# A state space layer with its chunk matrices read from a table of lags, turned states copied by ScalarE, and its output kept with channels on partitions

## What is computed

```python
def s5_bidirectional(u, a_re, a_im, log_dt, b_re, b_im, c_re, c_im, d_skip):
    # u: (B, S, 512) in 32 groups of 16 channels, 64 complex states per group, two directions
    y = ut * d_skip
    for d in range(N_DIRS):
        a_bar = exp(lam * dt); b_bar = B * (a_bar - 1.0) / lam
        bu = einsum('sbgc,gpc->sbgp', ut, b_bar)                       # complex
        _, xs = lax.associative_scan(_scan_op, (a_el, bu), reverse=(d == 1), axis=0)
        y = y + einsum('sbgp,gcp->sbgc', real(xs), c_re[d]) - einsum('sbgp,gcp->sbgc', imag(xs), c_im[d])
    return y
...
        y = jax.nn.gelu(y)
        y = y * jax.nn.sigmoid(jnp.einsum('bsc,ce->bse', y, w_glu[l]) + b_glu[l])
        ssm = y * jax.nn.silu(z_ssm)
        merged = jax.nn.sigmoid(g_attn) * jnp.einsum('bsc,cd->bsd', attn, w_branch_attn[l]) \
               + jax.nn.sigmoid(g_ssm) * jnp.einsum('bsc,cd->bsd', ssm, w_branch_ssm[l])
```

## Time and profile before

| | us |
|---|---|
| median of three runs | 4124.12 (4119.46 to 4124.37) |
| profiled execution | 4137.53 |
| its span | 4135.7 |
| TensorE busy in the span | 3700.5 |
| loop over groups (`te_s5`) | 420.9 to 1111.6 |
| transposes and gate (`te_glu`) | 1111.6 to 1176.5 |
| branch products (`te_br`) | 1554.9 to 1777.0 |

### The profile page before, as it was taken

One profiled execution on the slowest core, in us unless ns is written; L12 is line 12 of the kernel. 1 busy time (PEld: TensorE's weight loads), 2 busy tenths in 40 slices (PEclk: granted clock), 3 DMA queues, 4 the chain that ended last, 5 costly groups with the idle time before them and its releaser, 6 DMA issues. The chain is left out here.

```text
span 4135.7 us, 35726 instructions
## 1 busy us (share of the span) xinstructions
PE 3700.5 (89%) x12787; PEld 2003.3 (48%) x12787; DVE 1692.5 (41%) x4152; ACT 1021.0 (25%) x2529; POOL 1003.2 (24%) x1396
## 2 busy tenths in 40 slices
PE   4999999999999889989999967888879973899997
PEld 3744666666545544444444444445545541444443
DVE  4766232233354572336655555333333341112211
ACT  3211111111210450012344444333212210222221
POOL 0377774000000680000000024544420003111111
PEclk8999999999999999999999988999989986999999
DMA  3234423222154003222310000001002213999997
GB/s 140 74 132 150 140 102 115 91 74 74 63 191 138 31 11 127 76 92 72 113 34 23 11 6 1 1 0 62 1 33 92 82 62 120 313 314 327 330 316 232
DMA packets 116436, 450.87 MB, mean 109 GB/s; under 512 B 25587, under 2 KB 40435, under 8 KB 104732
## 3 DMA queue, kind: packets, MB, share of 16 engines
q1 hardware_dynamic: 91324, 360.91, 24.4%
q0 software_dynamic: 19456, 67.15, 5.8%
q10 hardware_dynamic: 5472, 20.45, 1.4%
HBM read 335.10 MB, written 113.36 MB: 108 GB/s over the span
## 5 line engine op out<-in xcount | busy, mean ns | idle before, releaser
L140 PE MATMUL pst<-arena 128*128 128x512 f32 (+3 forms) x6618 | 2710.3, 567 | 97.4 <-DVE arena L156 35.4
L140 PEld LDWEIGHTS pst<-arena 128*128 128x128 f32 x6618 | 1248.7, 200 | 1430.1 <-issue 1270.4
L145 PE MATMUL pst<-arena 128*128 128x128 f32 x2211 | 336.3, 292 | 203.5 <-DVE arena L244 52.5
L162 POOL TENSOR_TENSOR arena<-arena 128x128 f32<-128x128 f32 (+7 forms) x880 | 429.5, 488 | 70.1
L162 DVE TENSOR_TENSOR arena<-arena 128x1 f32<-128x1 f32 (+8 forms) x1185 | 402.2, 339 | 83.3 <-ACT arena L2175 22.6
L145 PEld LDWEIGHTS pst<-arena 128*128 128x128 f32 x2211 | 271.2, 149 | 335.4 <-issue 117.0
L1228 POOL TENSOR_SCALAR arena<-arena 128x384 f32<-128x384 f32 (+1 forms) x128 | 151.8, 1205 | 703.3 <-DVE arena L1220 703.0
L151 ACT ACTIVATE arena<-pst,arena 128x128 f32<-128x128 f32 (+1 forms) x630 | 246.5, 486 | 157.8 <-PE pst L145 155.1
L2122 POOL TENSOR_SCALAR arena<-arena 128x512 f32<-128x512 f32 (+3 forms) x160 | 216.5, 1374 | 281.0 <-DVE arena L162 252.3
L2229 PE MATMUL pst<-arena 128*128 128x256 f32 (+1 forms) x576 | 155.0, 393 | 83.1 <-ACT arena L150 42.5
L165 DVE TENSOR_SCALAR arena<-arena 128x1 f32<-128x1 f32 (+10 forms) x569 | 141.7, 249 | 186.0 <-DMA arena<-in_bc 71.6
(11 more groups left out here) (197 smaller groups left out, 2403.9 us busy)
## 6 DMA issues: line engine op xcount, KB each, us to landing
arena<-in_w_exp SPq DMA_DIRECT2D x48, 3072.0 KB, 12.3
arena<-in_w_ada SPq DMA_DIRECT2D x48, 512.0 KB, 4.9
rotd<-arena POOLq DMA_DIRECT2D x32, 512.0 KB, 4.0
arena<-rotd SPq DMA_DIRECT2D x32, 512.0 KB, 4.5
arena<-sgd SPq DMA_DIRECT2D x16, 1024.0 KB, 8.3
arena<-pwd SPq DMA_DIRECT2D x32, 432.0 KB, 3.5
pwd<-arena SPq DMA_DIRECT2D x16, 576.0 KB, 5.0
h2d<-arena SPq DMA_DIRECT2D x17, 512.0 KB, 2.9
```

Source lines behind the costliest of these rows:

```text
L140: x = t.do.matmul(o, l, r, start=(i == 0), stop=(i == len(pairs) - 1))
L145: x = t.do.transpose(o, i, ident[0:i.shape[0], 0:i.shape[0]])
L162: own(v, s).tensor_tensor(o, a, b, op).then_inc(*inc(s, *event))
```

## The change

Five things.

1. **M from a table of lags.** M depends on the distance of two tokens only. For each four groups `te_lag` makes the 16x16 blocks of all distances with eight matmuls (128 moving columns, output 16 x 128), ScalarE and VectorE copy and add them (`ac_lag`, `ve_lag`), SP stores 16 x 240 values per group in `hkd`, and eight loads with overlapping rows read M back (`sp_s5_blocks`). The first seven calls stand among the first 32 projection tiles, after the tiles in `LAG_AT`; the eighth opens `te_s5`. The 16 small matmuls of each group, the padded B with its store and loads, and Ms are gone.
2. **Turned states by ScalarE.** `te_s5_states` makes two products of 256 columns; ScalarE copies the bank with its halves exchanged (`ac_s5_turned`, two copies of 64 partitions x 512).
3. **Output with channels on partitions.** `te_s5_out` has M, CA and QA as the stationary operand and 256 chunks as columns: five matmuls. Gelu runs on each group's 128 x 256 (`ac_s5_out`), SP stores it in `ytd` and loads it back so that a partition holds a channel, with its tokens ordered (t, n): 8 tokens of a chunk outermost, 256 chunks innermost. The 64 transposes and 16 strided copies of the gate are gone.
4. **Reading that layout.** The gate and the branch product take their 512 moving columns as `by_token`: 64 chunks x 8 tokens, the tokens innermost, 256 elements (1024 bytes) apart. VectorE's last pass of the gate reads yT and writes ssmT in the same pattern.
5. **Order.** The group loop is shifted so that the states of g + 1 are made before the output of g. Three table buffers instead of two. The gate goes by token range first (`u, m = n // 4, n % 4`), and its last pass waits for the four gate tiles of its range, since ssmT lies over yT.

```diff
+LAG_AT = [0, 2, 6, 12, 17, 22, 27]
...
+        def te_lag(t, q4):
+            CAs, b1 = CA2[q4 % 2], b1s[q4 % 2]
+            t.wait_ge(*at("mat_ve", "QA", q4))
+            t.wait_ge(*(at("lag_ac", "H", q4 - 1) if q4 else at("u_ac", "Ug", 30)))
+            t.wait_ge(*at("lag_ve", "H", q4 - 1))
+            for g in range(4):
+                for d in range(2):
+                    x = t.do.matmul(bank(d)[0:16, g * 128:(g + 1) * 128], b1[:, 2 * g + d, :],
+                                    CAs[:, g, 160 * d:160 * d + 128], start=True, stop=True)
+            x.then_inc(*inc("lag_pe", "H", q4))
...
-                b1, b2, x2 = Bb[:, 0, :, :], Bb[:, 1, :, :], Bb[:, 2, :, :]
+                CAs, b1, b2, x2 = CA2[q4 % 2], b1s[q4 % 2], Bb[:, 0, :, :], Bb[:, 1, :, :]
+                v.wait_ge(*at("lag_pe", "H", q4 - 2))
+                if q4 == 1:
+                    v.wait_ge(*at("u_pe", "Ug", 30))
...
+            for k in range(8):
+                src = bass.AP(tensor=hkd.tensor, offset=4 * q4 * 3840 + 112 - 16 * k, ap=[[240, 16], [3840, 4], [1, 128]])
+                s.do.dma_start(Mq[q4 % 2][16 * k:16 * k + 16], src).then_inc(*dma(f"ld_m{q4 % 2}", "M", q4))
...
-            for s in range(8):
-                t.do.matmul(bank(0)[:, 16 * s:128], Bpad[i][:, 0, 112 - 16 * s:240 - 16 * s],
-                            CA[:, 0, 0:128 - 16 * s], start=(s == 0), stop=False)
-            for s in range(8):
-                x = t.do.matmul(bank(0)[:, 0:16 * (s + 1)], Bpad[i][:, 1, 112 - 16 * s:240 - 16 * s],
-                                CA[:, 1, 128 - 16 * s:144], start=False, stop=(s == 7))
...
-                t.do.matmul(bank(2 + d)[:, 0:256], BPT[i][:, d, 0:128], u_, start=True, stop=True)
-                t.do.matmul(bank(2 + d)[:, 256:512], BPT[i][:, d, 128:256], u_, start=True, stop=True
-                            ).then_inc(*inc("s5_pe", "v", g, d))
+                x = t.do.matmul(bank(2 + g % 2)[:, 256 * d:256 * d + 256], BPT[g % 2][:, d, :], u_, start=True, stop=True)
...
+            mm(t, y_bank(g), [(Mq[g // 4 % 2][:, g % 4, :], Ug[:, g, :])] +
+               [(A_[:, d, lo:lo + 128], Gs[:, r, d, d:d + 256])
+                for d, lo in ((0, 16), (1, 0)) for r, A_ in enumerate((CA, QA))]).then_inc(*inc("s5_pe", "y", g))
...
+        def sp_s5_channels(s, g):
...
+            s.do.dma_start(yT[m][p:p + 16], ytd[g].rearrange("(t c) n -> c t n", t=8)).then_inc(*dma("ld_yT", "yT", g))
...
+        def by_token(x, u):
+
+            return x[:, :, 64 * u:64 * u + 64].rearrange("p t n -> p n t")
...
-                mm(t, bank(4 + u), [(w3[:, k, m * 128:(m + 1) * 128], yT[:, k, u * 512:(u + 1) * 512])
-                                    for k in range(4)]).then_inc(*inc("glu_pe", "glu", n))
+                mm(t, in_chunks(bank(4 + m)), [(w3[:, k, m * 128:(m + 1) * 128], by_token(yT[k], u)) for k in range(4)]
+                   ).then_inc(*inc("glu_pe", "glu", n))
...
-                tt(v, "glu_ve", o, o, yT[:, m, us], MUL)
                 v.wait_ge(*at(f"ld_z{n % 2}", "zs", n))
-                tt(v, "glu_ve", o, o, stg[n % 2], MUL, "ssm", n)
+                tt(v, q, o, o, stg[n % 2], MUL)
+                v.wait_ge(*at("ld_yT", "yT", G - 1))
+                v.wait_ge(*at("glu_pe", "glu", 4 * u + 3))
+                tt(v, q, by_token(ssmT[m], u), in_chunks(o), by_token(yT[m], u), MUL, "ssm", n)
...
-                    mm(t, bank(2 * u + 1), [(BW[d % 2][:, 4 + k, :], ssmT[:, k, us]) for k in range(4)]
+                    mm(t, in_chunks(bank(2 * u + 1)), [(BW[d % 2][:, 4 + k, :], by_token(ssmT[k], u)) for k in range(4)]
```

More of the change, by code:

```diff
@@ L581, in pw_stored @@
         def pw_stored(e, q4):
-            for k in range(4):
+            for k in range(3):
                 e.wait_ge(*at(f"st_pw{k}", "pw", q4))
@@ new lines, in ac_lag, with ve_lag @@
+        def ac_lag(a, q4):
+            o = Hs[q4 % 2]
+            two = [bank(d)[0:16, :].rearrange("p (g n) -> p g n", g=4) for d in range(2)]
+            a.wait_ge(*at("lag_pe", "H", q4))
+            a.wait_ge(*at("u_pe", "Ug", 30))
+            a.wait_ge(*at("st_hk", "H", q4 - 2))
+            a.do.activation(o[:, :, 112:240], two[0], ACT.Copy).then_inc(*inc("lag_ac"))
+            a.do.activation(o[:, :, 0:112], two[1][:, :, 0:112], ACT.Copy).then_inc(*inc("lag_ac", "H", q4))
+        def ve_lag(v, q4):
+            q, o = "lag_ve", Hs[q4 % 2][:, :, 112:128]
+            v.wait_ge(*at("ld_sgn", "dcol"))
+            tt(v, q, dd, bc(ident[0:16, 0:16], 1, [16, 4, 16]), bc(dcol[0:16, 4 * q4:4 * q4 + 4], 2, [16, 4, 16]), MUL)
+            v.wait_ge(*at("lag_ac", "H", q4))
+            tt(v, q, o, o, bank(1)[0:16, :].rearrange("p (g n) -> p g n", g=4)[:, :, 112:128], ADD)
+            tt(v, q, o, o, dd, ADD, "H", q4)
@@ L655, in ve_mat @@
                     tt(v, q, o, o, x_, SUB, *(["QA", q4] if d == 1 else []))
+                if q4:
+                    ve_lag(v, q4 - 1)
         def po_rot(p):
@@ L789, in te_s5_out @@
         def te_s5_out(t, g):
-            i = g % 2
             _, CA, QA = pw_views(g)
-            t.wait_ge(*at("s5_ve", "M", g))
+            t.wait_ge(*at(f"ld_m{g // 4 % 2}", "M", g // 4))
             t.wait_ge(*at("s5_ve", "G", g))
-            t.wait_ge(*(at("s5_ac", "Y", g - 1) if g else at("u_ac", "Ust", 12)))
-            for h in range(2):
-                o = bank(4)[:, h * 128:(h + 1) * 128]
-                t.do.matmul(o, Ug[:, g, h * 128:(h + 1) * 128], Ms[i], start=True, stop=False)
-                for d, lo in ((0, 16), (1, 0)):
-                    for r, A_ in enumerate((CA, QA)):
-                        x = t.do.matmul(o, Gs[:, r, d, h * 128 + d:h * 128 + d + 128], A_[:, d, lo:lo + 128],
-                                        start=False, stop=(d == 1 and r == 1))
@@ L832, in te_s5 @@
         def te_s5(t):
+            te_lag(t, 7)
             te_s5_first(t, 0)
@@ L877, in sp_s5 @@
         def sp_s5(s):
-            sp_s5_load(s, 0)
-            sp_s5_load(s, 1)
+            for g in range(3):
+                sp_s5_pw(s, g)
+                if g < 2:
+                    sp_s5_rot(s, g)
+            sp_lag(s, 7)
+            sp_s5_blocks(s, 0)
             for n in LATE[0]:
@@ L2765, in tensor @@
                 te_proj(t, n)
+                if n in LAG_AT:
+                    te_lag(t, LAG_AT.index(n))
             te_s5(t)
```

289 lines of the change are left out of this document (145 added, 144 removed).

## The result

| | before | after |
|---|---|---|
| median | 4124.12 (4119.46 to 4124.37) | 4183.16 (4175.88 to 4197.16) |
| profiled execution | 4137.53 | 4179.35 |
| its span | 4135.7 | 4177.6 |

The changed kernel is slower: the ratio is 1.015, with a 95% interval of 1.0121 to 1.0179. The median of after is of four executions.

The account below looks back on a forecast made before the run. TensorE's own stream was taken to bound the kernel; loop -144, table of lags +20, strided reads +64 and +128, gate ends +3 and +8 gave +79 on 4124, so 4203 us, range 4075 to 4235.

Parts of the forecast that it names:

- The strided reads: Gate and branch matmuls reading 1024 bytes apart: 1.0 us more each, +64 us for the gate and +128 for the branch.
- the sum: Whole kernel: all terms added, -144 + 20 + 64 + 128 + 3 + 8 = +79 us.
- The moving stream that keeps its pace: Rival, gate and branch: strided reads cost nothing extra, the 192 us fall away, total 4011; chance 0.16.
- reads half as slow: Rival, gate and branch: part of the read delay overlaps the array's work, total 4107; chance 0.14.
- lines far apart cost more: Rival, gate and branch: 1024-byte steps cost more than 32-byte ones, total 4395; chance 0.03.
- The late tables: Rival, before the loop: VectorE's table steps grow and TensorE waits, 5 to 10 us on top; no separate chance.
- The loop: Group loop: fewer TensorE matmuls save 4.50 us a group, -144 us for 32, new period 17.0 us.
- The table of lags: First tiles to loop: 64 added matmuls, waits for VectorE's tables and the handover, +20 us (14 to 30).
- The ends of the gate: Before and behind the gate: TensorE waits for weights, +3 us at the head and +8 at the other end.
- The head: Before the gate: TensorE idles for its weights and comes back at the lower clock, +3 us.

Follow-up runs that it names:

- step1: Kernel after with gate, its last VectorE pass and branch product reading 512 tokens contiguously, in wrong order; 0.433 us a record, total not comparable.
- step8: Kernel after with gate and branch moving operands read 8 elements (32 bytes) apart, last VectorE pass contiguous, wrong token order; 0.927 us a record, total not comparable.
- keep: Kernel after with only the table of lags and turned states kept; output, transposes, gate and branch as before; 4011.9 us, ratio to before 0.9718.
- keep_tab: As keep, but VectorE's wait for the end of te_u stands before the first write of CA, not the whole step; 4000.78 us, ratio to before 0.9688.

## Why the prediction was right, and where its numbers were off

**The strided reads** decided, as the sum had it, and `step1` shows that the reads are what costs. Their size was off: the term is "500 ns a record, two records a matmul, 1.0 us on top of 0.86". Measured are 0.88 (1.74 to 1.745 against 0.86), +56 and +112 instead of +64 and +128. The row it came from, the weight load of 315 ns in the earlier trace rows, has a step of 32 bytes; at just that step the moving operand gave (0.927 - 0.433) / 512 = 0.96 ns a column against the row's 0.98, and 0.86 at 1024 bytes. That is 24 of the 25 us between +79 and +54; the other misses cancel.

The mechanism is another than the sum's, though. The sum adds a delay to the array's time. If that were so, a record would cost more at the lower clock, where the array's own part is longer: by an estimate from the rows below 0.86 + 0.44 = 1.30 us instead of 0.87. Weight loads stand one to a record, so their distance is that of the records. At the start of the gate the granted clock is 0.50, here for after (length, then busy time of TensorE, its weight loads, VectorE, ScalarE, GpSimd, clock, DMA share, GB/s):

```profile
1004.33:1007.10 2.77, 2.77 (x4) 1.13 (x5) 0.00 (x0) 0.00 (x0) 0.00 (x0) 0.50 0.18 70
```

TensorE's weight loads in that stretch of after:

```profile
1006.23 0.31 PEld L143 LDWEIGHTS pst<-arena 128*128 128x128 f32 x1 [0.55 <-issue]
1007.10 0.31 PEld L143 LDWEIGHTS pst<-arena 128*128 128x128 f32 x1 [0.55 <-issue]
```

The same in `step1`, whose reads are contiguous (clock 0.50 from 1008.83 to 1012.83 us):

```profile
1010.69 0.34 PEld L143 LDWEIGHTS pst<-arena 128*128 128x128 f32 x1 [0.52 <-issue]
1011.55 0.34 PEld L143 LDWEIGHTS pst<-arena 128*128 128x128 f32 x1 [0.52 <-issue]
```

A contiguous record costs 0.86 us at 0.50 and 0.43 at 1.00; a strided one costs 0.87 at both, and in `step8` 0.92 at both. So the strided reads have a pace of their own, and the array's time lies beneath it, whole, at either clock. The delay is not added to it. That the weight load's delay per column, added on, gave nearly the right time at the full clock is in part luck: nothing here shows that the two delays are one thing. A strided load takes 315 / 128 = 2.46 ns a column, a strided moving record 0.927 / 512 = 1.81.

**The rivals.** The moving stream that keeps its pace, and reads half as slow, are out by the measured 1.745 us a matmul. The reason given against the first, that the moving stream has no cover, is not what the trace shows: the array's work is covered by the reads, which are the longer of the two. The rival that lines far apart cost more was not only absent, the sign was the other one (0.872 against 0.927). The late tables came true, inside the range, with 9 us more than the sum had.

**The loop** came out at -146.4 for -144, the period at 16.98 for 17.0. ScalarE, VectorE and SP had the slack that the earlier trace rows promised.

**The table of lags** cost +28.7 instead of +20. Eight products at 1.85 us are 14.8, as forecast. The waits are 1.86 + 7.23 + 1.70 = 10.8 instead of about 5.6, and the product that follows the 7.23 us of idleness took 3.36 instead of 1.92, at a granted clock of 0.50 to 0.56. These make 27 of the 28.7. The mis-sized term is "33 us" for VectorE's step of four groups. In VectorE's timeline of after the work on the second and on the third tables begins 239.60 - 202.86 = 36.7 us apart:

```profile
202.86 23.77 DVE L165 TENSOR_TENSOR arena<-arena 128x128 f32<-128x128 f32 x25 [13.12 <-PE pst L148]
...
238.39 1.08 DVE L168 TENSOR_SCALAR arena<-arena 128x128 f32<-128x128 f32 x3 [11.21 <-DMA arena<-in_bc]
239.60 23.68 DVE L165 TENSOR_TENSOR arena<-arena 128x128 f32<-128x128 f32 x25
```

Both parts of the step grew against the earlier trace rows: the work from 21.7 to 23.7, the waiting for inputs from 9.2 to 11.2. The prediction moved VectorE's step by 12.7 us and left its length as it was. But at its new place it runs beside other work of GpSimd. `ve_lag` did fall into the waiting (226.73 to 227.19 us in VectorE's timeline of after). The work grew beside GpSimd's wide passes, as above in `keep`. The waiting grew because the stores of the tables landed late: in SP's timeline of after `in_bc` is issued at 235.88, 9.35 us behind the first store of that step, where it was 6.58 before, and SP had waited 5.5 us of that for `pwd` to land. The DMA issues of after, 225 to 237 us, with the median time to landing:

```profile
pwd<-arena SPq DMA_DIRECT2D x2, 576.0 KB, 7.6
rotd<-arena POOLq DMA_DIRECT2D x2, 512.0 KB, 4.2
```

The two large stores of before landed in 4.7 us. In after 1 MB of GpSimd's rotations, issued at 225.39, goes out beside them. The store of H, new in this queue, is not the cause: it stands there in `keep_tab` too, and there the two land in 4.7 us and `in_bc` is issued 221.24 - 215.01 = 6.23 us behind the first store. That it is the meeting with the rotations is read from these rows; no run tried it alone.

**The ends of the gate.** The end came out at +7.1 for +8, by the chain as forecast: passes held until gate tile 15, then the issue of `in_w_q`, then its landing. SP's timeline of after shows the load issued 3.7 us behind the gate's end:

```profile
1119.26 0.43 SPq L1040 DMA_DIRECT2D arena<-in_w_q  x1
```

The head was -0.8 instead of +3. TensorE stood idle 8.92 us as forecast, and the clock did fall, as shown above: 0.50 (the lower of the levels 1.2 and 2.4 GHz) in the first 2.77 us, 1.00 again from 1010 on.

```profile
1010.00:1115.00 105.00, 105.00 (x122) 24.84 (x120) 26.06 (x38) 10.32 (x15) 0.00 (x0) 1.00 0.09 30
```

But the lower clock cost the strided reads nothing: 0.87 us a record there, and 111.27 / 128 = 0.869 over the whole gate. With contiguous reads after the same idle time, in `step1`, the gate took 57.97 us instead of 55.17 and did lose 2.8. I had charged a price of contiguous matmuls to strided ones.

## What to carry to other kernels

Before a transpose is removed by reading its source with a step, multiply the columns that the step will be read with by how often they are read: here 9.8 us of transposes stood against 168 us, because the gate reads each element in four matmuls and the branch in eight. On TensorE a moving operand of float32 with a step of two elements is nearly free; four or more double a stream of 512-column matmuls at the full clock; a layout that is read often is better turned once, as before did in its 16 copies out of PSUM. And a step that moves in time doesn't keep its length: ask which work of other engines, and which of their transfers, it will run beside at its new place.

## What the hardware showed that I had not expected

- The price of a moving operand's step jumps between 8 and 16 bytes (0.453 to 0.903 us a record of 512 columns) and is slightly lower at 256 and 1024 bytes (0.868, 0.872) than at 32 (0.927, 0.922).
- After 8.92 us of idleness, at a granted clock of 0.50, strided records followed each other at 0.87 us, as at 1.00; contiguous ones took 0.86 instead of 0.43 and the gate lost 2.8 us by it. Where the reads set the pace, TensorE's clock does not.
- VectorE's passes of 128x576 last 758 ns beside narrow passes of GpSimd and 1275 beside its passes of 128x512, which themselves last 1475.
- On VectorE the multiply with a strided operand and a strided result lasts 1.04 us, the contiguous one of the same size 0.69. The rows are from VectorE's timeline of after, at the end of the gate:

```profile
1115.64 1.04 DVE L165 TENSOR_TENSOR arena<-arena 128x512 f32<-128x512 f32 x1 [17.74 <-PE pst L143]
...
1119.40 0.69 DVE L165 TENSOR_TENSOR arena<-arena 128x512 f32<-128x512 f32 x1 [0.20 <-DMA arena<-zsd]
```
